# Routing in even shares over both token blocks, exponentials in the routing's own quad, condition products on other stages

## The reference

```
q = (t @ w_query).reshape(T, 8, 2, 128);  s = einsum('thpd,pnd->thpn', q, sub_keys)
top_s, top_i = top_k(s, 16)                        # in each of the two halves
cand = top_s[..., 0, :, None] + top_s[..., 1, None, :]   # 256 candidates
best_s, best_pos = top_k(cand, 16);  gates = softmax(best_s)
act = gelu(einsum('td,ted->te', t, expert_u[experts]))   # 128 experts a token
out = einsum('te,ted->td', gates * act, expert_v[experts])
```

## Time and profile before

| what | value |
| --- | --- |
| span of the profiled execution | 3307.9 us |
| its time | 3309.74 us |
| median of three other runs | 3306.81 us |
| busy: PE, DVE, POOL, ACT | 91%, 71%, 39%, 31% of the span |
| granted TensorE clock, mean | 0.956 |
| moved by DMA | 993.59 MB, mean 300 GB/s |

### The profile page before, as it was taken

How to read it: one execution, slowest core, us unless ns; L and a number is a source line. 1 busy time by engine, 2 the same in 40 slices (tenths; PEclk the granted TensorE clock), 3 DMA queues, 4 the chain that set the end, 5 groups by cost and what they waited for, 6 DMA issues and landing times. The chain is left out here.

```text
span 3307.9 us, 43537 instructions
## 1 busy us (share of the span) xinstructions
PE 2996.9 (91%) x15744; PEld 2396.8 (72%) x15744; DVE 2357.4 (71%) x4777; ACT 1019.1 (31%) x2038; POOL 1283.0 (39%) x1194
## 2 busy tenths in 40 slices
PE   8999899897787899979998899959999999999999
PEld 5877566564554587757666676729997999996898
DVE  5866888876656688698996766586654787856574
ACT  2322322210221232232211100035455544444543
POOL 1105677777667211466776766660000010000000
PEclk9999899998898899989999899979999999999999
DMA  8759999999999877899999999994561787742353
GB/s 342 243 179 351 345 409 404 407 409 408 383 345 379 312 246 288 322 342 409 409 404 409 394 409 409 409 364 151 183 226 46 245 276 245 255 163 92 117 183 103
DMA packets 273765, 993.59 MB, mean 300 GB/s; under 512 B 31648, under 2 KB 32448, under 8 KB 273296
## 3 DMA queue, kind: packets, MB, share of 16 engines
q0 software_dynamic: 170960, 625.89, 49.1%
q1 hardware_dynamic: 100944, 361.15, 30.8%
q10 hardware_dynamic: 1648, 3.78, 0.3%
HBM read 989.61 MB, written 1.05 MB: 299 GB/s over the span
## 5 line engine op out<-in xcount | busy, mean ns | idle before, releaser
L290 PE MATMUL bank<-hT,ring 128*128 128x256 f32 x3744 | 840.8, 383 | 16.2 <-ACT hT L930 13.1
L290 PEld LDWEIGHTS bank<-hT,ring 128*128 128x128 f32 x3744 | 716.7, 192 | 146.7 <-issue 34.3
L416 POOL DMA_INDIRECT gring<-in_expert_u,idx x512 | 597.2, 1166 | 328.8 <-issue 149.1
L416 POOL DMA_INDIRECT gring<-in_expert_v,idx x512 | 597.1, 1166 | 290.6 <-issue 154.4
L586 PE MATMUL bank<-gring,dg 128*128 128x512 f32 x1012 | 528.4, 667 | 149.5 <-DMA gring<-in_expert_v,idx 111.8
L1383 DVE CUSTOM_DVE_ANT_0 gring<-gring,t_tok 128x1024 f32<-128x1024 f32 x512 | 601.7, 1222 | 28.3 <-DMA gring<-in_expert_u,idx 22.3
L1690 DVE TENSOR_TENSOR wl<-ring,wr 128x1024 fp32r<-128x1024 f32 x309 | 377.8, 1224 | 219.1 <-ACT wr L1685 218.6
L586 PEld LDWEIGHTS bank<-gring,dg 128*128 128x128 f32 x1012 | 207.8, 213 | 408.5 <-issue 355.8
L1354 DVE SCALAR_TENSOR_TENSOR x<-gring,wts,x 128x1024 f32<-128x1024 f32 x259 | 332.8, 1285 | 235.6 <-DMA gring<-in_expert_v,idx 162.9
L1694 PE MATMUL bank<-hr,wr 128*128 128x258 f32 (+1 forms) x1512 | 430.0, 284 | 1.5 <-DVE hl L2156 0.7
L1696 PE MATMUL bank<-hr,wl 128*128 128x258 f32 (+1 forms) x1512 | 426.7, 282 | 0.0
(11 more groups left out here) (327 smaller groups left out, 3862.7 us busy)
## 6 DMA issues: line engine op xcount, KB each, us to landing
ring<-in_stream SPq DMA_DIRECT2D x679, 512.0 KB
t_tok<-in_ada POOLq DMA_DIRECT2D x56, 512.0 KB, 5.7
gring<-in_ada POOLq DMA_DIRECT2D x56, 512.0 KB, 5.5
lat_ada<-in_ada POOLq DMA_DIRECT2D x48, 512.0 KB, 5.3
gring<-in_expert_u,idx POOLq DMA_INDIRECT x512
gring<-in_expert_v,idx POOLq DMA_INDIRECT x512
na_bias_sb<-in_na_bias POOLq DMA_DIRECT2D x1, 4096.0 KB, 15.9
x<-in_x SPq DMA_DIRECT2D x2, 512.0 KB, 4.3
```

The costliest lines, as they stand in the source:

```text
L290: last = pe.matmul(out, w[:, k * P:(k + 1) * P], act_T[:, k, :], start=(k == 0), stop=(k == KD - 1))
L416: pool.indirect_dma_start(out=gring[:, N % GR, :], out_offset=None, in_=table, in_offset=bass.IndirectOffsetOnAxis(ap=idx[:, b, 4 * (Q % 3 ...
```

## The change

Routing of (b, h) is now the (8b + h)-th; quads 4i and 4i+1 route head i+1 for all i to 14, so block 1 is routed in quads 28 to 57. The exponential is in quad 4i+1. Quads 0, 2 and 4 are one query head earlier on ACT, and quad 0's sum on PE. ACT takes block 1's norm squares and the first exponential ahead of query unit 2. Of layer 1's condition units 18 are for the context alone; their latent products move to the second block's first FFN, with POOL loads and a third part of `MOD_PARTS`. Layer 1's condition vectors are loaded and go through silu in the last two quads of layer 0.

```diff
-WEIGHTS_AT, SUM_AT = {1: 0, 2: 1, 4: 2, 5: 3, 7: 4}, {2: 0, 4: 1, 6: 2, 7: 3}
+WEIGHTS_AT, SUM_AT = {0: 0, 2: 1, 3: 2, 5: 3, 6: 4}, {1: 0, 4: 1, 6: 2, 7: 3}
 ADA = ([(0, i, (LAT, CTX)) for i in range(48)],
-       [(0, i, (LAT, CTX)) for i in range(48, 72)] + [(1, i, (LAT, CTX)) for i in range(24)] +
-       [(1, i, (CTX,)) for i in range(24, 40)])
-ADA_LATE = [(1, i, (LAT,)) for i in range(24, 72)]
+       [(1, i, (LAT, CTX)) for i in range(24)] + [(0, i, (LAT, CTX)) for i in range(66, 72)] +
+       [(0, i, (CTX,)) for i in range(48, 66)] + [(1, i, (CTX,)) for i in range(24, 40)])
+ADA_LATE = ([(0, i) for i in range(48, 66)], [(1, i) for i in range(24, 72)])
 def route_at(b, h):
-    if b == 0:
-        return max(0, 2 * h - 1)
-    return min(2 * h + 2, 2 * PH - 1)
+    return PH * b + h
...
         def scalar(act):
-                if L:
-                    act.wait_ge(xg, 4 * L)
...
+                if L == 0:
+                    act_condition(act, 0)
...
                 for t in range(2 * EARLY_HEADS):
+                    if t == 2:
+                        act_norm_squares(act, z + 1, [1])
+                        act_route_exp(act, L, 0, 0)
...
-                act_norm_squares(act, z + 1, [1])
-                act_route_exp(act, L, 0, 0)
...
                     if Q == QUADS - 2:
...
+                        if L + 1 < DEPTH:
+                            act.wait_ge(c_res, 16)
+                            act_condition_in(act)
                     if Q == QUADS - 1:
+                        if L + 1 < DEPTH:
+                            act_condition(act, L + 1)
...
         def act_gather(act, L, Q):
-            if Q < QUADS // 2 + 1:
-                if Q % 4 == 2 and Q < 28:
-                    act_route_exp(act, L, 0, Q // 4 + 1)
-                if Q % 4 == 0 and Q:
-                    act_route_exp(act, L, 1, Q // 4 - 1)
+            nb, nh = divmod(Q // 4 + 1, PH)
+            if Q % 4 == 1 and nb < NB:
+                act_route_exp(act, L, nb, nh)
...
         def dve_gather(dve, L, Q, before, after):
-            h = Q // 4
-            if Q < 32:
-                if Q % 4 == 0 and h < 7:
-                    dve_route_first(dve, L, 0, h + 1)
-                if Q % 4 == 1 and h < 7:
-                    dve_route_second(dve, L, 0, h + 1)
-                if Q % 4 == 2:
-                    dve_route_first(dve, L, 1, h)
-                if Q % 4 == 3:
-                    dve_route_second(dve, L, 1, h)
+            nb, nh = divmod(Q // 4 + 1, PH)
+            if nb < NB:
+                if Q % 4 == 0:
+                    dve_route_first(dve, L, nb, nh)
+                if Q % 4 == 1:
+                    dve_route_second(dve, L, nb, nh)
...
         def vector(dve):
-                    dve_ada(dve, L, 5)
+                    dve_ada(dve, L, 5 + 2 * L)
...
-                dve_ada(dve, L, 4 + 2 * L)
+                dve_ada(dve, L, 5)
...
                     elif 8 <= n < 16:
-                        dve_ada(dve, L, 2)
+                        dve_ada(dve, L, 1 + (L and n >= 10))
...
         def late_loads(pool):
+            for part in range(2):
+                if part:
+                    pool.wait_ge(sp_used, split_before["up1"])
+                pool.dma_start(lat_ada[:, 3, :], io["cond"][LAT]).then_inc(lat_cond_in, 16)
+                for i, (layer, t) in enumerate(ADA_LATE[part]):
...
+                if part == 0:
+                    pool.wait_ge(sp_used, S0[0] + 3 * KF)
+                    pool.dma_start(na_bias[:], io["na_bias"]).then_inc(bias_in, 16)
...
         def dve_ffn(dve, F):
+                if F == 0 and 4 <= m < 22:
+                    dve_lat_ada(dve, 0, m - 4)
```

More of the change, by code:

```diff
@@ L1041, in act_ctx, with act_condition_in, act_condition @@
                 yield from act_ctx_kv(act)
+        def act_condition_in(act):
+            for i in range(2):
+                act.dma_start(cond[i], io["cond"][i]).then_inc(cond_in, 16)
+        def act_condition(act, L):
+            act.wait_ge(cond_in, 32 * (L + 1))
+            for i in range(2):
+                act.activation(cond[i], cond[i], ACT.Silu).then_inc(silu_done, 1)
         def scalar(act):
@@ L1054, in scalar @@
                     act_norm_squares(act, z)
-                for i in range(2):
-                    act.dma_start(cond[i], io["cond"][i]).then_inc(cond_in, 16)
-                if L:
+                    act_condition_in(act)
+                else:
                     act_norm_squares(act, z, [1])
                 act_norm_evac(act, z, one["norm1_g"][:, L], range(min(L, 1), NB))
-                act.wait_ge(cond_in, 32 * (L + 1))
-                for i in range(2):
-                    act.activation(cond[i], cond[i], ACT.Silu).then_inc(silu_done, 1)
+                if L == 0:
+                    act_condition(act, 0)
                 for b in range(NB):
@@ L1248, in program @@
         MOD_PARTS = ([(0, 0, (LAT, CTX)), (0, 1, (LAT, CTX))],
[L1249 removed]
+                     [(0, 2, (CTX,)), (1, 0, (LAT, CTX)), (1, 1, (CTX,))],
+                     [(0, 2, (LAT,))],
                      [(1, 1, (LAT,)), (1, 2, (LAT,))])
@@ L1386, in dve_gather @@
                 dve_route_gates(dve, L, 0, 0)
[L1387 to L1390, removed]
+            if Q % 4 == 2 and nb < NB:
+                dve_route_gates(dve, L, nb, nh)
             if Q % 4 == 0:
-                dve.wait_ge(rt_fin, 2 * (16 * L + route_at(b, h % 8)) + 2)
+                dve.wait_ge(rt_fin, 2 * (16 * L + Q // 4) + 2)
             if Q:
@@ L1608, in late_loads @@
                 pool.dma_start(late[name][:], io[name]).then_inc(late_in, 16)
-            pool.wait_ge(sp_used, S0[0] + 3 * KF)
-            pool.dma_start(na_bias[:], io["na_bias"]).then_inc(bias_in, 16)
-            pool.wait_ge(sp_used, split_before["up1"])
-            pool.dma_start(lat_ada[:, 3, :], io["cond"][LAT]).then_inc(lat_cond_in, 16)
-            for i, (layer, t, _) in enumerate(ADA_LATE):
-                if i >= 3:
-                    pool.wait_ge(lat_ada_used, i - 2)
-                pool.dma_start(lat_ada[:, i % 3, :], io["ada"][layer * NMOD * KD + t]).then_inc(lat_ada_full[i % 3], 16)
+            for part in range(2):
[3 more added lines that the diff above has]
+                for i, (layer, t) in enumerate(ADA_LATE[part]):
+                    n = part * len(ADA_LATE[0]) + i
+                    if i >= 3:
+                        pool.wait_ge(lat_ada_used, n - 2)
+                    pool.dma_start(lat_ada[:, i % 3, :], io["ada"][layer * NMOD * KD + t]).then_inc(lat_ada_full[i % 3], 16)
+                if part == 0:
+                    pool.wait_ge(sp_used, S0[0] + 3 * KF)
+                    pool.dma_start(na_bias[:], io["na_bias"]).then_inc(bias_in, 16)
         def store(sp):
@@ L1785, in act_ffn, with dve_lat_ada @@
                     act_high(act, s0 + 48 + d)
-        def dve_lat_ada(dve, i):
-            layer, t, _ = ADA_LATE[i]
+        def dve_lat_ada(dve, part, i):
+            layer, t = ADA_LATE[part][i]
+            before = part * len(ADA_LATE[0])
             if i == 0:
-                dve.wait_ge(silu_done, 2 * DEPTH + 1)
-            dve.wait_ge(lat_ada_full[i % 3], 16 * (i // 3 + 1))
+                dve.wait_ge(silu_done, 2 * DEPTH + 1 + part)
+            dve.wait_ge(lat_ada_full[i % 3], 16 * (before // 3 + i // 3 + 1))
             w = lat_ada[:, i % 3, :]
@@ L1795, in dve_lat_ada @@
                                      accum_out=mods[:, layer, t, LAT:LAT + 1]).then_inc(lat_ada_used, 1)
-            if i == len(ADA_LATE) - 1:
-                dve.wait_ge(lat_ada_used, i + 1)
-                dve_mods(dve, MOD_PARTS[2])
+            if i == len(ADA_LATE[part]) - 1:
+                dve.wait_ge(lat_ada_used, before + i + 1)
+                dve_mods(dve, MOD_PARTS[2 + part])
         def dve_ffn(dve, F):
```

11 lines of the change are left out of this document (6 added, 5 removed).

## The result

| | before | changed |
| --- | --- | --- |
| median of 7 runs, us | 3301.38 | 3283.05 |
| lowest and highest, us | 3296.51, 3313.81 | 3277.80, 3285.63 |
| profiled execution: time (span), us | 3309.74 (3307.9) | 3279.74 (3277.6) |

The ratio is 0.9936 (95% interval 0.992 to 0.9953): 18.3 us less, where the prediction's sum had 12.5. Differences between those two traces are therefore some 12 us too large in sum (30 for 18.3).

The account below looks back on a forecast made before the run. DMA bandwidth of 404 to 409 GB/s bounds the gather, with PE and DVE full where its starts fall below; attention and second block are PE-bound. Terms -7 -7 +4 +1 -2 -2 +0.5 = -12.5 us gave 3294, range 3270 to 3316.

Parts of the forecast that it names:

- more than that: Rival: both gather starts fill up to the DMA ceiling, -36 us in all, 3271; chance 0.12.
- the term for the starts: Gather starts of both layers: -7 us each, 6 from routing spread and 1 from earlier exponential and gelu.
- Ceiling and missed time: Gather slices top out at 404 to 409 GB/s; starts miss up to 21.4 us in layer 0, 15.8 in layer 1.
- Why they filled: Gather starts: one head of routing less on full DVE in quads 6 and 7, -6 us each; exponential and slots 1.
- Second half: Routing moved into later quads, mostly into DVE's waits: +4 us in layer 0's context attention, +1 in layer 1.
- POOL and the shared port: Row fetches: routing doesn't visibly hold POOL, so no term; the skill's port rule only adds a little to the slower rival.
- Condition, layer 0: Layer 0's attention: PE's 2.43 us wait for DVE's weights goes, -2 us, bounds -3 and +6.
- Condition, layer 1, and the FFN: Layer 1's attention loses 18 latent products, -2 us, forget gate later; first FFN takes them, +0.5 us.
- Quad 0's earlier sum: PE's sum of quad 0 one head earlier might wait for rows: taken as 0, up to 5 us a layer.
- not as said: Rival: quad 0's exponential and gelu hold ACT, PE stands for rows, 5 us a layer, 3304; chance 0.05.
- Signs named in advance: No gates' wait over 2 us; DVE about 80%, rate above 360 at starts; quad 8 7 us earlier; 960-1020 at most 330.
- signs of being wrong: PE idle over 3 us before quad 0's sum; lower second-half rate in layer 1; forget-gate wait over 3; FFN PE below 82.

Follow-up runs that it names:

- u_spread: Changed kernel with the routing order of before, all heads done by quad 31; 3279.98 us, ratio 0.9936 to the kernel before.
- c_only: Kernel before with the condition part alone (18 latent products moved, new counts, layer 1's silu at layer 0's end); 3296.28 us, ratio 0.9984.
- u_slots: Changed kernel with the early places (WEIGHTS_AT, SUM_AT, norm squares, first exponential) as before; 3286.80 us, ratio 0.9953 to the kernel before.
- u_exp: Changed kernel with each exponential one quad later, after the routing's second part; 3288.77 us, ratio 0.9965 to the kernel before.
- b_l0: Kernel before with only layer 0's condition counts of the changed kernel; third chip, 3288.87 us, ratio 0.9990.
- n_neutral: Changed kernel with layer 0's first two condition units swapped, same instructions and bytes; third chip, 3293.05 us, ratio 1.0003 to the kernel before.
- h_hold: Changed kernel with POOL's fifth row fetch waiting for query units 0 and 1; third chip, 3298.40 us, ratio 1.0017 to the kernel before.
- u_l1: Changed kernel with layer 1 and the first FFN as before, layer 0's new counts kept; third chip, 3295.68 us, ratio 1.0014 to the kernel before.
- u_cond: Changed kernel with all condition units as before in both layers, only layer 1's silu kept at layer 0's end; 3295.45 us, ratio 0.9980.
- c_l0: Changed kernel with layer 0's condition counts as before; second chip, 3298.43 us, ratio 0.9996 to the kernel before.
- e_tight: Changed kernel with block 1 routed in quads 28 to 43, two heads in four quads; 3297.44 us, ratio 0.9980 to the kernel before.

## Why the prediction was right, and where it was not

The number was right (3294 forecast, range 3270 to 3316, measured 3283), the direction too. It lies 1 us outside the 3284 to 3304 that the prediction gave its own mechanism, halfway between that forecast and the rival "more than that" (3271). That the term for the starts came near is luck: the cause named for it brings nothing, and the one priced at 1 us brings it. Of its steps:

- **Ceiling and missed time**: right. The starts were where bytes were missing, and they filled. From the first value fetch of quad 0 to that of quad 8 the traces have 127.8 us before and 117.0 after in layer 0, 122.9 and 114.6 in layer 1: -10.8 and -8.3 for -7 and -7, within the bounds. The stall described below lies in these lengths; without it they are 120.6 and 113.3, and 119.2 and 110.4: -7.3 and -8.8.
- **Why they filled**: wrong, and this is the step that failed ("I take -6 in each", for one head of routing less in quads 6 and 7, with 1 us for exponential and slots). u_spread puts that head back and keeps the starts (117.5 and 114.4 us); c_only, with neither early slots nor early exponentials, does not fill them (126.7 and 124.9). With the old slots it is 118.6 and 118.9, with late exponentials 117.1 and 117.9. The stall does not make this difference: without it c_only has 121.5 and 119.3, u_spread 114.0 and 111.0, u_slots 114.2 and 112.7, u_exp 112.1 and 109.7. The gates' waits of 9.5 us were in the path after all, and in the even order either edit alone takes most of them away (in the old order only both together were tried). That holds for the first two chips. On the third the waits are there in b_l0 (12.4 and 9.9 us in layer 0) and gone in n_neutral, and the starts differ by only 0.9 and 3.6 us (123.4 and 122.5, 121.6 and 118.0), because a wait before quad 0's sum takes 5 to 6 of it back. I had argued that the rows of quads 4 and 5 and ACT's next gelu stood so close behind them that 1 us would be left.
- **Second half**: layer 0's +4 is about right as a sum, -2.6 + 4.1 + 2.4 = +3.9 over quads 8 to 58 by the table, but not as to its place: only 2.4 of it stands in quads 44 to 57, for which it was forecast, and the single traces of the two orders overlap there. The working had a slip that the rounding hides: 6.0 less 3.8 is 2.2 and not 2.3. Layer 1's +1 was too small: -1.9 + 4.3 + 0.9 = +3.3. So the spread by itself costs some 7 us over quads 8 to 58, and its relief of quads 0 to 8 pays nothing back (u_spread's trace is 5 us shorter than the changed kernel's; its ratio is the same). Rows in both orders move at 403 GB/s in layer 1's quads 28-44, so the 4.3 there may be bytes of the weight stream that the quicker first half left over; the sum over 8 to 58 is the sounder number.
- **POOL and the shared port**: the mean fetch fell by 0.02 us in both first halves and rose by 0.01 and 0.03 in the second. Over quads 44 to 57 of layer 1 it is 1.178 us in the four alternate traces and 1.227 in the nine even ones (one of these, n_neutral, has 1.187, less than the 1.193 of c_only). The rule of the Trainium skill that I set against the trace (SBUF — State Buffer, "Who interferes with whom") agrees in sign with these. The long fetches are not routing's in the main, though: in the traces before and changed a fetch whose first 0.94 us fall on an idle DVE takes 0.94 us (300 fetches, none over 1.05), one beside the dot products alone 1.45 to 1.48 in the mean. The price, 112 x 0.05 = 5 us of POOL, lies where POOL waits anyway, and the stretch of layer 1 is 0.9 us longer.
- **Condition, layer 0**: -2 forecast. The two waits of PE, 1.08 and 2.43 us, went, and the first fetch is 3.5 to 5.8 us earlier in all eleven kernels with the new counts, 0 to 0.4 in the two others; timed alone, -3.1 us (b_l0, interval 0.3 to 5.9).
- **Condition, layer 1, and the FFN**: -2 and +0.5 forecast; u_l1 against n_neutral gives 2.6 us together. The forget gate's wait came (2.85 us in the changed kernel), as said.
- **Quad 0's earlier sum**: I took 0 and kept 5 us a layer. It is 0 in layer 0 of the changed kernel's own trace: PE comes to that sum at 267.6, after a stall, and the rows are there. On the third chip it is 9.17 less 3.90, 5.3 us in layer 0, and 8.7 less 2.9, 5.8 in layer 1. The rival "not as said" had this size, and it is what the third chip shows.
- **Signs named in advance**: quad 8 came 10.8 us earlier against quad 0 for 7; DVE stood at 89 and 80% for about 80; the rate at 358 and 366 for above 360; 960-1020 did not fall to 330. Of the signs of being wrong one shows faintly: the rate in layer 1's second half, 405 before, is 401.

What the prediction did not have is the stall at the query stage's start, between the end that PE's records give its first full query unit and the release of ACT and SP. It is 3.4 to 9.3 us long in the twenty layers of the ten traces taken before the third chip, 1.7 or less in the eight on it. Before pays 7.2 + 3.7 us of it there and the changed kernel 3.7 + 4.2. Where it is missing, before is 11.5 to 12.2 us faster, about the 10.9 that it pays. The twin of the changed kernel should then be 7.9 us faster, and it is 10.0 slower: the early sum's wait (9.2 and 8.7 us) comes in the stall's place. The stall's cause is open. The traces settle that the release is late and not ACT; h_hold, meant to test the row fetches as the cause, ran on a chip without the stall. For layer 0 u_l1 tells that n_neutral's lost gain is the chip's and not the swap's. Why chips differ is not shown. Of u_cond's and c_l0's 10 to 15 us some 4.4 are accounted for by the first fetch; 5.0 and 4.4 us more go with the stall in u_cond's one trace, and most of c_l0's are in no trace at all.

No kernel beat the changed one clearly. u_spread had its ratio with the routing order of before, and b_l0 was the only one faster than before on the third chip. So the 18.3 us were measured where before takes 3301; where it takes 3292, what was run speaks for no gain.

## What to carry to other kernels

A wait that seems shadowed by a neighbour is worth testing before it is priced at nothing: here two small edits on ACT freed 7 to 10 us of each gather start on two chips, and the large one beside them none. Taking work out of a stretch where an engine looks full pays nothing if the path runs through another wait. Work put where the DMA engines are at their limit is not free either: by the table a head of routing, 8.3 us of DVE, costs 0.2 to 1.4 us (2.6/5, 4.1/3 and 2.4/4 in layer 0; 1.9/5, 4.3/3 and 0.9/4 in layer 1). A longer stretch is a loss only if the next one does not give it back, as it did in e_tight. A gain of half a per cent should be timed on a second chip, with a twin that changes nothing, before it is put down to an edit.

## What the runs showed of the hardware

The same kernel has a median of 3303.5 and 3304.2 us on two chips (26 and 23 runs) and of 3292.0 on a third (35 runs), at the same granted clock (0.954 to 0.963 in single runs on the two, 0.955 to 0.961 on the third).

In all ten traces of kernels taken before the third chip, PE's semaphore for the first full query unit steps 3.4 to 9.3 us after the end that its records give, and ACT and SP are released together at that moment; in the four traces of the third chip the step follows the record by 0.02 us. The DMA engines move some 410 GB/s in both cases (415 in the stall of before, 411 in n_neutral).

An indirect fetch of 128 rows occupies POOL for 0.94 us beside an idle DVE (300 fetches in the traces before and changed, none over 1.05). Beside the fused dot products alone, 128x1024 with both inputs in SBUF, the mean is 1.45 and 1.48 us, and 433 of 622 take over 1.05.
